# One Strassen level over 1024 tokens: the MLPs of two blocks run as one stage, their hidden values go through DRAM

## Chip, cores, metric

One core of a Trainium2 chip. The time is device microseconds of one launch (us below), median of the runs shown.

## What is computed

One layer of a decoder trunk on 2048 tokens of 1024 features, float32 throughout:

```
h = rms_norm(x, norm_mix);  m = rms_norm(mem, norm_mem)          # x: 2048 x 1024, mem: 256 x 1024
q, k, v, g_lr, r, xq = split(h @ w_in)                             # gated linear attention, 4 heads, chunked, causal
y_mix = rms_norm(attention(q, k, v, decay(g_lr)), out_gain) * silu(r)
y_mem = softmax attention of xq into the memory tokens
x = x + concat(y_mix, y_mem) @ w_out                               # 1536 -> 1024
u = relu(rms_norm(x, norm_mlp) @ w_up)                             # 1024 -> 4096
x = x + (u * u) @ w_down                                           # 4096 -> 1024
out = rms_norm(x, final_norm)
```

## The kernel before

The tokens are worked through in four blocks of 512 (`BLOCKS`, `BLOCK`). A block's **mixers** are the projections, the attention and the output projection; after them comes its **MLP**. All five engines have a program of their own, written out by hand in the order in which the work is to run; they meet at counting semaphores, and each engine takes its instructions strictly in that order. SyncE (SP) issues nearly all DMAs, also in a fixed order, so a DMA behind one whose semaphore is not there yet waits with it.

**Float32 products.** Each operand is split in a high part (`_hi`, ScalarE, ACT below, copies it to the matmul's format) and a low part (`_lo`, VectorE, DVE below, subtracts). A product is then three matmuls, hi x hi, hi x lo, lo x hi (`product`, lines 3026 to 3028). Weights come from DRAM into the two slots of `raw` and are split into the two slots of `w_hi`, `w_lo`.

**Strassen.** With one level of Strassen (Winograd's form) a product of matrices cut in quarters is seven products M1 to M7 of quarters instead of eight. `PRODUCTS` says which operands each takes (A11, A12, A22 and the sums S1 to S4 on the left, B11, B21, B22 and the sums T1 to T4 on the right). M6 is accumulated on M1 in the same PSUM bank, M7 on M6, M4 on M7, and M3 on M5, so a bank has to be read out before the product that goes on in it may start: `empty` is that wait of TensorE (PE below), on `bank_read`.

**The MLP before.** For block 0 `h @ w_up` is done in 16 plain chunks of 256 hidden features (`MLP`, `UPS`). For blocks 1 to 3, 4 chunks are plain and 12 go by Strassen on quarters of 256 tokens ("up a", "up b" in `LATE_MLP`, banks from `late_bank`), which makes matmuls of 256 columns. The hidden values stay on the chip: they are squared, their Strassen sums made (`u_parts`) and split (`u_hi`, `u_lo`), and after each 4 chunks the seven down products of that group follow, by Strassen, in matmuls of 512 columns, each added to `xres` at once (line 2621). The weight sums T1 to T4 of `w_down` are made on the way (`weight_sums`, lines 2087 to 2090) and kept in DRAM (`w_mix`), as are those of `w_up` (`w_up_mix`). The output projection is plain in block 0, by Strassen in the others.

## Time and profile before

| what | value |
|---|---|
| time, median of 3 runs (lowest to highest) | 2464.06 us (2461.39 to 2465.43) |
| span of the profiled execution, first to last instruction | 2459.9 us |
| PE busy | 2441.6 us, 12912 instructions |
| DVE busy | 1830.7 us |
| ACT busy | 1291.8 us |
| DMA moved | 505.00 MB |

The profiled execution has no other time of its own than its span; the 4.2 us from it to the median lie before the first and after the last instruction. An engine's busy time leaves out its waits. A matmul's duration in the profile runs on into the next one's (the array is pipelined), so what one costs PE is read from the distance of starts.

### The profile page before, as it was taken

To read this page: it belongs to the slowest core of one execution; us is meant where nothing else is said; L and a number is where in the kernel's file an instruction comes from. 1 tells how busy PE (TensorE), PEld (TensorE's weight loads), DVE (VectorE), ACT (ScalarE), POOL (GpSimd) and SP (SyncE) were. 2 spreads that over 40 slices of the span, in tenths; PEclk is the share of its full clock that TensorE was granted. 3 is DMA by queue.
4 is the path that set the end of the run, shared out by engine and by line. 5 is a ranking of instruction groups with operands and counts; after the bars stand their busy time and mean duration, and the time that the engine had idled before them with its cause. 6 is when DMAs were issued, how large, how long until landed. Compare 5 with 4: busy or idle time off the path is not lost.

```text
span 2459.9 us, 34497 instructions
## 1 busy us (share of the span) xinstructions
PE 2441.6 (99%) x12912; PEld 2105.9 (86%) x12912; DVE 1830.7 (74%) x2671; ACT 1291.8 (53%) x2035; POOL 312.5 (13%) x327
## 2 busy tenths in 40 slices
PE   9999999999999999999999999999999999999998
PEld 8888888888788888889988888898898888889987
DVE  6677468778856788777775768877785677887777
ACT  5545354544543456566644345665665435556655
POOL 0033200000303320000020431000020142000000
PEclk9999999999999999999999999999999999999999
DMA  8964548677695444466564626355665553545554
GB/s 317 350 213 172 188 172 313 251 274 258 244 373 211 171 163 133 163 214 209 188 219 175 242 101 202 111 184 203 213 212 203 189 199 122 184 149 177 188 182 179
DMA packets 237843, 505.00 MB, mean 205 GB/s; under 512 B 12432, under 2 KB 125456, under 8 KB 219504
## 3 DMA queue, kind: packets, MB, share of 16 engines
q1 hardware_dynamic: 237248, 502.73, 58.4%
q8 instruction: 105, 1.72, 0.3%
q14 instruction: 58, 0.48, 0.1%
q10 hardware_dynamic: 432, 0.07, 0.0%
HBM read 423.07 MB, written 79.69 MB: 204 GB/s over the span
## 4 chain that ended last, share of the span: by engine, by line
PE 95%; DVE 2%; DMA 2%; issue 1%; ACT 0%; POOL 0%; SPq 0%; DVEq 0%; POOLq 0%; ACTq 0%
PE banks L3026 28%; PE banks L3028 28%; PE banks L3027 28%; PE banks L3216 3%; PE banks L3188 1%; PE banks L3262 1%; PE banks L3256 1%; PE banks L3165 1%; PE banks L3240 1%; DMA sr<-in_w_out 1%; PE banks L3178 0%; PE banks L3482 0%; PE banks L3274 0%; DMA xres<-in_x 0%; PE banks L3099 0%
## 5 line engine op out<-in xcount | busy, mean ns | idle before, releaser
L3026 PE MATMUL banks<-h_hi,w_hi 128*128 128x512 f32 (+1 forms) x1728 | 605.6, 350 | 2.4 <-DMA w_lo<-w_in_lo 0.8
L3028 PE MATMUL banks<-h_hi,w_lo 128*128 128x512 f32 (+1 forms) x1728 | 598.1, 346 | 0.0
L3027 PE MATMUL banks<-h_lo,w_hi 128*128 128x512 f32 (+1 forms) x1728 | 597.9, 346 | 0.0
L2833 DVE TENSOR_TENSOR w_lo<-raw,w_hi 128x1024 fp32r<-128x1024 f32 (+1 forms) x312 | 364.8, 1186 | 56.7 <-ACT w_hi L1861 56.4
L1861 ACT ACTIVATE w_hi<-raw 128x1024 fp32r<-128x1024 f32 (+1 forms) x312 | 300.9, 1003 | 166.7 <-PE banks L3026 59.4
L3026 PEld LDWEIGHTS banks<-h_hi,w_hi 128*128 128x128 f32 x1728 | 327.3, 189 | 44.1 <-issue 3.1
L3028 PEld LDWEIGHTS banks<-h_hi,w_lo 128*128 128x128 f32 x1728 | 327.2, 189 | 40.6
L3027 PEld LDWEIGHTS banks<-h_lo,w_hi 128*128 128x128 f32 x1728 | 327.5, 190 | 39.3
L3026 PE MATMUL banks<-w_hi,u_hi 128*128 128x512 f32 x896 | 350.8, 392 | 1.3 <-ACT w_hi L1401 1.0
L3028 PE MATMUL banks<-w_hi,u_lo 128*128 128x512 f32 x896 | 348.8, 389 | 0.0
L3027 PE MATMUL banks<-w_lo,u_hi 128*128 128x512 f32 x896 | 348.7, 389 | 0.0
L2621 DVE TENSOR_TENSOR xres<-banks,xres 128x512 f32<-128x512 f32 x274 | 180.4, 683 | 63.2 <-PE banks L3028 58.8
L3026 PEld LDWEIGHTS banks<-w_hi,u_hi 128*128 128x128 f32 x896 | 168.2, 188 | 40.0 <-issue 4.0
L3028 PEld LDWEIGHTS banks<-w_hi,u_lo 128*128 128x128 f32 x896 | 168.2, 188 | 35.3
L3027 PEld LDWEIGHTS banks<-w_lo,u_hi 128*128 128x128 f32 x896 | 168.2, 188 | 35.0 <-issue 0.7
L2113 DVE TENSOR_TENSOR w_lo<-raw,w_hi 128x1024 fp32r<-128x1024 f32 x116 | 150.0, 1328 | 30.9 <-ACT w_hi L1401 29.3
L1265 POOL TENSOR_TENSOR rstd<-ms,minus_half 128x1 f32<-128x1 f32 x44 | 26.9, 617 | 1146.6 <-DVE ms L2128 1142.2
L2106 DVE TENSOR_TENSOR w_lo<-raw,w_hi 128x2048 fp32r<-128x2048 f32 x47 | 107.7, 2291 | 55.8 <-ACT w_hi L1394 54.8
L1291 POOL TENSOR_TENSOR queries<-q,query_dec 128x384 f32<-128x384 f32 x144 | 120.8, 865 | 182.4 <-ACT query_dec L1557 94.9
L2744 DVE TENSOR_TENSOR u_lo<-u_parts,u_hi 128x768 fp32r<-128x768 f32 (+1 forms) x128 | 135.1, 1092 | 0.8 <-ACT u_hi L1822 0.8
L1401 ACT ACTIVATE w_hi<-raw 128x1024 fp32r<-128x1024 f32 x80 | 81.4, 1053 | 97.6 <-DMA raw<-w_out_mix 31.0
L3026 PE MATMUL banks<-w_hi,h_hi 128*128 128x512 f32 x312 | 126.0, 404 | 1.2 <-ACT v L1527 0.8
(311 smaller groups left out, 4392.9 us busy)
## 6 DMA issues: line engine op xcount, KB each, us to landing
raw<-w_mix SPq DMA_DIRECT2D x52, 1024.0 KB, 4.8
raw<-in_w_down SPq DMA_DIRECT2D x48, 1024.0 KB, 5.7
raw<-w_up_mix SPq DMA_DIRECT2D x72, 512.0 KB, 4.8
w_hi<-w_in_hi SPq DMA_DIRECT2D x29, 1024.0 KB, 4.9
w_lo<-w_in_lo SPq DMA_DIRECT2D x29, 1024.0 KB, 7.9
raw<-in_w_up SPq DMA_DIRECT2D x28, 1024.0 KB, 5.6
raw<-in_gla_w_in SPq DMA_DIRECT2D x21, 1024.0 KB, 7.5
raw<-in_w_up SPq DMA_DIRECT2D x36, 512.0 KB, 4.1
```

The source lines that it names most:

```text
L1291: last = nc.gpsimd.tensor_tensor(kind_cols(queries, w, kind), spans(at_chunk(q, c), w, first, count), kind_cols(query_dec, w, kind), ALU.mult)
L1401: nc.scalar.activation(w_hi[:, i % 2, at], raw[:, i % 2, at], ACT.Copy).then_inc(hi_split.sem, 1)
L1861: nc.scalar.activation(w_hi[:, i % 2, at], raw[:, i % 2, at], ACT.Copy).then_inc(hi_split.sem, 1)
L2106: nc.vector.tensor_tensor(w_lo[:, i % 2, :], raw[:, i % 2, :], w_hi[:, i % 2, :].bitcast(F32), ALU.subtract).then_inc(lo_split.sem, PIECES)
L2113: nc.vector.tensor_tensor(w_lo[:, i % 2, at], raw[:, i % 2, at], w_hi[:, i % 2, at].bitcast(F32), ALU.subtract).then_inc(lo_split.sem, 1)
L2621: nc.vector.tensor_tensor(xres[:, t, cols], bank(name), xres[:, t, cols], ALU.add)\
L2744: nc.vector.tensor_tensor(u_lo[:, c % ring(n), at, :], source, u_hi[:, c % ring(n), at, :].bitcast(F32), ALU.subtract).then_inc(u_ready.se ...
L2833: nc.vector.tensor_tensor(w_lo[:, i % 2, at], raw[:, i % 2, at], w_hi[:, i % 2, at].bitcast(F32), ALU.subtract).then_inc(lo_split.sem, 1)
L3026: after_chunk(pe.matmul(to, left[0], right[0], start=start, stop=False, skip_group_check=goes_on))
L3027: pe.matmul(to, left[0], right[1], start=False, stop=False, skip_group_check=goes_on)
L3028: return pe.matmul(to, left[1], right[0], start=False, stop=stop, skip_group_check=goes_on)
L3216: ins = pe.matmul(bank(name)[:, at:at + cols], keys[:, h, :], queries[:, h, 0:cols], start=True, stop=True)
```

## The change

The program is rewritten around the MLP. The mixers of blocks 0 and 1 now run one after the other, then one MLP for their 1024 tokens; then the same for blocks 2 and 3 (`MLPS` = 2). What it does, part by part:

- **Up.** All 16 chunks go by Strassen, a quarter being 512 tokens x 512 inputs x 128 features, so each of the seven products is 12 matmuls of 512 columns. `UP_STEPS` lists the 112 products (steps): for chunks 0 to 2 first M1 and M2 of each, then M5, M6, and M7, M3, M4; from chunk 3 on M1, M2, M5, M6, M7, M3, M4 of one chunk. The banks are in `up_bank`. The weights' sums are made on the chip from the raw chunk (`up_sum`), each operand is split into one of 8 places (`RING`), five steps ahead.
- **u.** ACT copies M1, M6 and M5 out of their banks (`keep_part`), DVE adds M2, M3 and M7 (`add_part`); relu and square of the three kept quarters is one `scalar_tensor_tensor` each, max(u, 0) * u (`kept_quarters`); the fourth is relu and square on ACT (`last_quarter`). DVE makes S1 to S4 (`u_sums`). All seven operands of the chunk go to DRAM (`u_kept`).
- **Down.** Seven products over all 4096 hidden features in four quarters (`DOWN_STEPS`, 28 steps of 48 matmuls of 512 columns). Each step loads 1 MB of weights and 1 MB of u and splits both.
- **w_down's sums.** 32 halves (`half_mix`) are loaded, summed by DVE between the steps of the first MLP's up part (`DOWN_MIX_AT`) and stored. `w_up_mix` is gone.
- **Mixers.** Block 0's output projection goes by Strassen too. The even block's rows wait in DRAM (`x_kept`), its normed columns too (`h_kept`).

Names in the program rows below: `banks` is PSUM, `s1`..`s4` the sums of h, `part_a`, `part_b`, `part_c`, `gain_fin` the places of a chunk's kept parts.

**PE, before, from the end of M6 (`s2`) to the start of M7 (`s3`) in a Strassen up chunk of blocks 1 to 3:**

```order
L3027 MATMUL banks<-s2_lo,w_hi 128x256
L3028 MATMUL banks<-s2_hi,w_lo 128x256
L3026 MATMUL banks<-s1_hi,w_hi 128x256 [waits bank_read1,s_lo_ready]
...
L3028 MATMUL banks<-s1_hi,w_lo 128x256
L3026 MATMUL banks<-s3_hi,w_hi 128x256 [waits s_lo_ready,bank_read0,lo_split,hi_split]
L3027 MATMUL banks<-s3_lo,w_hi 128x256
```

**PE, after, the same place in a chunk from 3 on:**

```order
L2918 MATMUL banks<-s2_hi,w_hi 128x512
L2919 MATMUL banks<-s2_lo,w_hi 128x512
L2920 MATMUL banks<-s2_hi,w_lo 128x512
L2918 MATMUL banks<-s3_hi,w_hi 128x512 [waits bank_read0,up_lo,up_hi]
L2919 MATMUL banks<-h_lo,w_hi 128x512
L2920 MATMUL banks<-s3_hi,w_lo 128x512
```

Before, M5's 12 matmuls in bank 1 stand between M6 and M7, which share bank 0. Now M7 follows M6 in one bank, and its first matmul waits for one more read of that bank than M6's did, which is ACT's copy of M6.

**DVE, after, at the start of an MLP** (the first row is the sum S1 of h; its waits are for the last transposed columns of h):

```order
L2731 TENSOR_TENSOR s1_sum<-columns_late,a22_sum 128x2048 [waits bank_read2,bank_read3,bank_read5,bank_read4,bank_read7,bank_read6]
L2704 TENSOR_TENSOR w_lo<-third_raw,w_hi 128x512 [waits up_hi]
L2731 TENSOR_TENSOR columns_late<-columns_early,columns_late 128x2048 [waits s_sum_ready,even_low]
L2731 TENSOR_TENSOR columns_early<-s1_sum,columns_early 128x2048 [waits s_sum_ready]
L2704 TENSOR_TENSOR w_lo<-third_raw,w_hi 128x512 [waits up_hi]
L2698 TENSOR_TENSOR third_raw<-third_raw 128x4x128 [waits up_sum_ready] x2
L2749 TENSOR_TENSOR part_a<-banks,part_a 128x512 [waits bank_read0,bank_full6]
L2704 TENSOR_TENSOR w_lo<-raw,w_hi 128x512 [waits up_hi]
L2698 TENSOR_TENSOR raw<-raw 128x4x128 [waits up_sum_ready] x2
L2742 TENSOR_TENSOR s1_lo<-s1_sum,s1_hi 128x2048 [waits s_sum_ready,s_hi_ready]
```

Three sums of 2048 elements now stand ahead of the first add, chunk 0's M2 out of bank 6; chunk 2's M2, the sixth product of the stage, takes bank 6 again. The low part of S1, for the seventh product, comes behind that.

**DVE, after, in the first MLP's up part, between a chunk's add of M2 and its add of M7:**

```order
L2761 SCALAR_TENSOR_TENSOR u<-part_c 128x512 [waits bank_read3]
L2761 SCALAR_TENSOR_TENSOR u<-gain_fin 128x512 [waits bank_read0]
L2096 TENSOR_TENSOR half_mix<-half_mix 128x256 [waits half_mix_loaded0]
L2097 TENSOR_TENSOR half_mix<-half_mix 128x256 [waits dve_step]
L2098 TENSOR_TENSOR half_mix<-half_mix 128x256
L2099 TENSOR_TENSOR half_mix<-half_mix 128x256 [waits dve_step]
L2704 TENSOR_TENSOR w_lo<-raw,w_hi 128x512 [waits up_hi]
L2698 TENSOR_TENSOR raw<-raw 128x4x128 x2
L2773 TENSOR_TENSOR u<-u 128x512 [waits u_sums_stored,relu_ready,square_ready]
L2774 TENSOR_TENSOR u<-u 128x512 [waits dve_step]
L2775 TENSOR_TENSOR u<-u 128x512
L2776 TENSOR_TENSOR u<-u 128x512 [waits dve_step]
```

The squares and sums of the chunk before and a weight sum of `w_down` (four operations) stand in one line with the reads of PSUM.

The diff, cut to its core:

```diff
-PRODUCTS = [("M1", A11, B11, 2, True, (0, 0)), ("M5", S1, T1, 4, True, (1, 1)), ("M6", S2, T2, 2, False, (0, 1)),
...
-LATE_UP_A = (("M1", A11, 0), ("M2", A12, 1), ("M6", S2, 2), ("M5", S1, 3))
-LATE_UP_B = (("M7", S3, 1), ("M3", S4, 0), ("M4", A22, 2))
+MLPS = BLOCKS // 2
+FIRST_UPS = 3
+UP_ORDER = ("M1", "M2", "M5", "M6", "M7", "M3", "M4")
+UP_STEPS = [(c, name) for c in range(FIRST_UPS) for name in ("M1", "M2")]
+UP_STEPS += [(c, name) for name in ("M5", "M6") for c in (2, 1, 0)]
+UP_STEPS += [(c, name) for c in (2, 1, 0) for name in ("M7", "M3", "M4")]
+UP_STEPS += [(c, name) for c in range(FIRST_UPS, UPS) for name in UP_ORDER]
...
+UP_LEAD = 5
...
+UP_ENDS = {15: 2, 20: 1, 25: 0, 30: 3, 36: 4, **{UP_AT[c, "M4"] + 1: c for c in range(5, UPS)}}
+S_SUMS_AT = {0: (S1,), 1: (S3, S2), 3: (S4,)}
+S_LOWS_AT = {2: S1, 4: S2, 5: S3, 7: S4, 9: A22}
...
+DOWN_MIX_AT = {18 + 5 * j // 2: j for j in range(DOWN_MIX)}
...
+def up_bank(c, name):
+    if name == "M2":
+        return 6 + c % 2
+    turn = c if c < FIRST_UPS else (5 - c) % 3
+    return turn + (3 if name in ("M5", "M3") else 0)
...
+            def half_mix_load(j):
+                slot, c, half = j % 2, j // 2, slice(j % 2 * 256, (j % 2 + 1) * 256)
...
+                    sp.wait_ge(half_mix_stored[slot], 16 * (j // 2))
...
+                    if m == 0 and at + 3 in DOWN_MIX_AT:
+                        half_mix_load(DOWN_MIX_AT[at + 3])
+                    if m == 0 and at - 1 in DOWN_MIX_AT:
+                        half_mix_store(DOWN_MIX_AT[at - 1])
...
+                    for e, name in enumerate(("M2", "M3", "M7")):
+                        part = up_home(c, e)
+                        dve.wait_ge(*mlp_read(m, ("up", c, name)))
+                        made = nc.vector.scalar_tensor_tensor(out=u[:, e, :], in0=part, scalar=0.0, in1=part,
+                                                              op0=ALU.max, op1=ALU.mult)
...
+                for at, (c, name) in enumerate(UP_STEPS):
+                    for e in S_SUMS_AT.get(at, ()):
+                        s_sums(e)
+                    if at + UP_LEAD < len(UP_STEPS):
+                        up_low(m, at + UP_LEAD)
+                    if at in S_LOWS_AT:
+                        s_low(S_LOWS_AT[at])
+                    if name in ("M2", "M7", "M3"):
+                        add_part(c, name)
+                    if at - 1 in UP_ENDS:
+                        kept_quarters(UP_ENDS[at - 1])
+                    if at - 2 in UP_ENDS:
+                        u_sums(UP_ENDS[at - 2])
+                    if m == 0 and at in DOWN_MIX_AT:
+                        half_mix_sums(DOWN_MIX_AT[at])
+                kept_quarters(UPS - 1)
+                split_down(0)
+                u_sums(UPS - 1)
...
+            def up_product(s):
+                    c, name = UP_STEPS[s]
...
+                    pe.wait_ge(*mlp_empty(m, ("up", c, name)))
```

By kind, the built programs differ on PE in this: of the matmuls that an operand pair of the split products makes, 3408 have 256 columns before and none after, and the count of those with 512 columns rises by 1500. All other matmuls, the 2688 of the down products among them, keep their number and size.

## Rows read from the trace of the kernel before

**Rows 1.** The page: span, engines' busy time, engines on the chain that ended last.
```profile
span 2459.9 us, 34497 instructions
PE 2441.6 (99%) x12912; PEld 2105.9 (86%) x12912; DVE 1830.7 (74%) x2671; ACT 1291.8 (53%) x2035; POOL 312.5 (13%) x327
PE 95%; DVE 2%; DMA 2%; issue 1%; ACT 0%; POOL 0%; SPq 0%; DVEq 0%; POOLq 0%; ACTq 0%
```

**Rows 2.** Timeline of PE: start and duration in us, engine, line, what.
```profile
1099.71 0.39 PE L3026 MATMUL banks<-w_hi,u_hi 128*128 128x512 f32 x1
...
1102.89 0.39 PE L3028 MATMUL banks<-w_hi,u_lo 128*128 128x512 f32 x1
1103.11 0.28 PE L3026 MATMUL banks<-h_hi,w_hi 128*128 128x256 f32 x1
...
1113.07 0.28 PE L3028 MATMUL banks<-h_hi,w_lo 128*128 128x256 f32 x1
```

**Rows 3.** Timeline: a product's last matmul and the first read of its bank, twice.
```profile
1117.38 0.28 PE L3028 MATMUL banks<-s_hi,w_lo 128*128 128x256 f32 x1
...
1117.77 0.38 ACT L1877 ACTIVATE c_parts<-banks 128x256 f32<-128x256 f32 x1 [0.28 <-PE banks L3028]
...
2452.98 0.39 PE L3028 MATMUL banks<-w_hi,u_lo 128*128 128x512 f32 x1
...
2453.40 0.69 DVE L2621 TENSOR_TENSOR xres<-banks,xres 128x512 f32<-128x512 f32 x1
```

**Rows 4.** ACT reading PSUM: the group of 512 elements, and eight reads of 256.
```profile
L1520 ACT ACTIVATE xq_a<-banks 128x512 f32<-128x512 f32 x16 | 9.6, 598 | 56.3 <-PE banks L3028 56.3
...
944.70 3.03 ACT L1775 ACTIVATE h_hi<-banks,gain_mlp 128x256 fp32r<-128x256 f32 x8 [2.12 <-PE banks L3482]
```

**Rows 5.** Timeline: PE starting again behind a releaser, in brackets the idle time.
```profile
395.37 0.47 PE L3026 MATMUL banks<-w_hi,u_hi 128*128 128x512 f32 x1 [0.98 <-ACT w_hi L1401]
...
709.61 0.20 ACT L1527 ACTIVATION_READ_ACCUMULATOR v<-banks,neg_top 128x1 f32 x1
...
709.95 1.32 PE L3165 MATMUL banks<-kmT,xq_a 128*128 128x256 f32 x5 [1.55 <-ACT v L1527]
```

**Rows 6.** DVE by shape: count, busy us, mean ns, idle before.
```profile
L2833 DVE TENSOR_TENSOR w_lo<-raw,w_hi 128x512 fp32r<-128x512 f32 x36 | 24.5, 680 | 0.0
L2732 DVE TENSOR_TENSOR u_parts<-u_parts 128x256 f32<-128x256 f32 x64 | 26.7, 418 | 0.0
L2426 DVE SCALAR_TENSOR_TENSOR sr<-b,sr 128x512 f32<-128x512 f32 x16 | 10.8, 676 | 46.2 <-ACT sr L1620 46.2
L2363 DVE TENSOR_TENSOR v_s<-raw,v_s 128x2048 fp32r<-128x2048 f32 x4 | 9.1, 2282 | 0.0
```

**Rows 7.** Timeline of DVE: two splits of 1024, then operations of 512.
```profile
560.55 2.35 DVE L2113 TENSOR_TENSOR w_lo<-raw,w_hi 128x1024 fp32r<-128x1024 f32 x2
562.82 0.68 DVE L2087 TENSOR_TENSOR xin<-xin 128x512 f32<-128x512 f32 x1
563.53 0.69 DVE L2088 TENSOR_TENSOR xin<-xin 128x512 f32<-128x512 f32 x1
564.14 0.69 DVE L2089 TENSOR_TENSOR xin<-xin 128x512 f32<-128x512 f32 x1
```

**Rows 8.** Chain in order of time: the 16 transposes of one half of h.
```profile
935.43 1.75 PE banks L3482 x16
```

**Rows 9.** DMA issues: count, KB each, median us from issue to landing.
```profile
raw<-in_w_up SPq DMA_DIRECT2D x36, 256.0 KB, 2.8
w_up_mix<-gain_fin SPq DMA_DIRECT2D x11, 512.0 KB, 4.1
w_in_lo<-w_lo SPq DMA_DIRECT2D x13, 1024.0 KB, 11.2
```

**Rows 10.** Windows: us; PE, PEld, DVE, ACT, POOL busy; granted clock; DMA share, GB/s.
```profile
2456.00:2458.00 2.00, 0.00 (x0) 0.00 (x0) 1.41 (x2) 0.00 (x0) 0.00 (x0) 0.99 0.82 334
2458.00:2460.00 2.00, 0.00 (x0) 0.00 (x0) 0.00 (x0) 0.00 (x0) 0.00 (x0) 0.50 0.50 191
```

More of the change, by code:

```diff
@@ L281, in block_uses @@
         if hs < 8:
[L282 removed]
+            if hs // 2 % 2 == 0 and not v_by_sums(n):
                 for t in v_tiles(hs):
@@ L738, in build, with bank_count @@
         dve_step = sem("dve_step")
         ones_r = ones[:].bitcast(F32R)
-        def bank_count(n, name, more):
-            uses = layout(n).uses
-            bank, index = uses.place[name]
-            ahead = sum(layout(m).uses.count[bank] for m in range(n))
+        def bank_count(phase, name, more):
+            bank, index = USES[phase].place[name]
+            ahead = sum(USES[before].count[bank] for before in range(phase))
             return bank, EARLY.count[bank] + ahead + index + more
@@ L864, in mix_uses @@
         def mix_uses(j):
-            return sum(mix_slot(before) == mix_slot(j) for before in range(j))
-        def slot_uses(slot, n, steps=None):
-            return sum(mix_slot(j) == slot for j in range(steps or MIX_STEPS + (OUT_MIX if n else 0)))
-        def mlp_source(s):
-            if MLP[s][0] == "up":
-                return wup[:, :, FCOLS * MLP[s][1]:FCOLS * (MLP[s][1] + 1)], KD
-            g, operand = MLP[s][1], PRODUCTS[MLP[s][2]][2]
+            return sum(OUT_MIX_SLOT[before] == OUT_MIX_SLOT[j] for before in range(j))
@@ new lines, in slot_uses, with columns, up_load, up_parts @@
+        def slot_uses(slot):
+            return OUT_MIX_SLOT.count(slot)
+        def columns(b):
+            return columns_late if b == 2 else columns_early
+        def up_load(c):
+            return sum(up_slot(before) == up_slot(c) for before in range(c))
+        def up_parts(c):
+            return third_parts if c == 2 else raw_parts[:, c % 2]
+        def up_source(c, operand):
+            k, f = {B11: (0, 0), B21: (1, 0), B22: (1, 1), T1: (0, 0), T3: (0, 1), T2: (0, 0), T4: (1, 0)}[operand]
+            return up_parts(c)[:, KG * k:KG * (k + 1), f, :]
@@ new lines, in store_rows, with store_columns @@
+            def store_rows(n):
+                for pair in range(2):
+                    sp.wait_ge(*read(n, ("out", "M4", pair)))
+                sp.dma_start(x_kept[:, n % 2, :, :], xres[:]).then_inc(rows_stored.sem, 16)
+            def store_columns(n):
+                for half in range(2):
+                    for g in range(KD // 2):
+                        sp.wait_ge(*read(n + 1, ("kept hT", half, g)))
+                sp.dma_start(h_kept, columns_early[:]).then_inc(columns_stored.sem, 16)
@@ L2056, in _ @@
+                for t in range(TILES):
+                    act.wait_ge(*mlp_read(m, ("down", "M4", t)))
+                    if m < MLPS - 1:
+                        square(ends[1][:, t, :], "final", m, TILES + t)
                     else:
                         half_square(t, 0)
+            for n in range(BLOCKS):
+                mixers(n)
+                if n % 2:
+                    mlp(n // 2)
         @block.vector
@@ L2211, in _, with mixers @@
             dve.wait_ge(half_gain_ready, 1)
-            for n in range(BLOCKS):
-                c_mlp, chunks = enter_block(n)
-                c_out, c_r = layout(n).out, layout(n).r
+            def mixers(n):
+                enter(mixers_phase(n))
+                c_end, c_out, c_r = layout(n).end, layout(n).out, layout(n).r
                 def next_chunk(i):
-                    if n and c_out <= i + 1 < c_mlp:
+                    if i + 1 >= c_out:
                         split_lo_out(n, i + 1)
@@ L3010, in _ @@
+                restart()
+            for n in range(BLOCKS):
+                mixers(n)
+                if n % 2:
+                    mlp(n // 2)
         @block.tensor
```

2687 lines of the change are left out of this document (1236 added, 1451 removed).

## The prediction

> **What bounds the kernel now.** I read the page first, for who sets the end. PE is busy 2441.6 of 2459.9 us and 95% of the chain that ended last is PE [rows 1]; DVE has 74%, ACT 53%. So a change pays only through what PE has to do, and costs through every wait that it gives PE. There is little old waiting to win back: PE's own idle time is 18 us, of which about 7 us stand behind its last matmul, at 2452.98 [rows 1, 3]. Next I read PE's timeline for the price of a matmul, from start to start, since the durations overlap: 14 intervals of 512 columns take 1102.89 - 1099.71 = 3.18 us, 0.227 us each; 83 of 256 columns take 9.96 us, 0.120 us each [rows 2]. Two matmuls of 256 cost 0.240 us, so one of 512 is 5% cheaper than its halves.
>
> **Matmuls.** 3408 of 256 columns go: 3408 x 0.120 = 409.0 us. 1500 of 512 come: 340.5 us. The difference is **-68.5 us**. (In short: three quarters of the up part had the Strassen saving already, at half the width; the rest, and block 0's output projection, get it now.) PE would be busy for about 2373 us.
>
> The Trainium skill ("TensorE: Matmul & The Clock Gate", section "Wait — 56ns, not 53.3ns?") gives N / 2.4 GHz and some 2.5 ns on top for the distance of two starts: 215.7 ns for 512 and 109.2 ns for 256. By that the difference would be 323.6 - 372.2 = -48.6 us, and the total below 20 us higher, no change. By that rule the trace does not agree: the distances are 11 ns longer at either width, and that part falls away with each of 1908 matmuls fewer.
>
> **New wait 1: M7 behind M6 in one bank.** From chunk 3 on M7 goes on in the bank in which M6 has just ended, and ACT must copy M6 out in between (the program rows in the section on the change). Before, M5 stood there. From the start of M6's last matmul to ACT's copy: 1117.38 to 1117.77, 0.39, and with 512 columns 2452.98 to 2453.40, 0.42 us [rows 3]. The copy of 512 elements: 0.60 us [rows 4]. From ACT's end (709.61 + 0.20) to PE's start: 0.14 us [rows 5]. Such a first matmul lasts 0.47 for 0.39 us: 0.07 more [rows 2, 5]. Of the sum, 1.23, the usual 0.227 goes off: 1.0 us. It comes 13 times in each MLP: **+26 us**. Bounds: 0.85 us if the copy runs like the shortest reads of PSUM on ACT (3.03 / 8 = 0.38 us for 256 elements [rows 4] leaves little below 0.45 for 512), and 1.1 if ACT is just in another copy: 22 to 29 us.
>
> **New wait 2: the start of an MLP.** Take the start of the first product as 0; a product lasts 12 x 0.227 = 2.72 us. After two products PE makes the second half of h's columns, 16 transposes in 1.75 us [rows 8], from 5.4 on. ACT reads these banks, eight reads in 3.03 us [rows 4], until about 9.0. Only then may DVE start S1: 2048 elements, 2.28 us [rows 6], to 11.3. In DVE's order follow a split of 512 (0.6 by distance of starts, 562.82 to 564.14 is 0.61 to 0.71 [rows 7]), S3 and S2 (2 x 2.28), another split, two weight sums (1.33, as two operations of 512 [rows 6]): 18.4. Then the add of chunk 0's M2, out of bank 6, to 19.0. The sixth product, chunk 2's M2, wants bank 6 at 5 x 2.72 + 2.0 = 15.6 us: late by 3.5 us. It ends at 21.9; the seventh needs the low part of S1, which is behind one more split and two sums and itself takes 2.28: 23.2. Late again, 1.4 us. Together 4.9 us, two MLPs: **+9.8 us**. Bounds 0 (if ACT's reads and the split end so much earlier that the order slips in) and 8 us each (each of the 2048s at its dearest, and DVE not through with the mixers).
>
> **New wait 3: up to down.** Behind chunk 15's M3, DVE has the add (0.6), the three squares (3 x 0.61 = 1.83) and only then the first split of the down part, 2 x 1.135 us [rows 7]: with 0.5 for the start some 5.3 us. PE has only M4 in between and wants the first down product at 2.95: 2.3 us, twice: **+4.6 us**.
>
> **DVE in the first MLP's up part.** Per chunk DVE has 7 splits (4.2), 4 weight sums (2.55), 3 adds (1.8), 3 squares (1.83), 4 sums of u (2.66): 13.0 us in a period of 7 x 2.72 + 1.0 = 20.1. A half of w_down's sums is four operations of 256 elements, 0.42 busy in the mean [rows 6], between 0.34 and 0.455 by whether each waits for the one before: 1.59 us; 2.8 of them fall in a chunk: 17.5 us. That fits, 87%, but not at every place. Between the reads of M2 and M7 there can be the squares, two halves and u's sums: then M7's read is done at about 19.0 where PE wants that bank at 17.75, 1.3 us, and some 0.45 with one half. Averaged over the orders 0.8 us a chunk in 11 chunks: **+9 us**. Bounds 0 (the second MLP has none, and its chunks should show it) and 25 (1.3 us at both places in most of the chunks).
>
> **What lies hidden.** A down step is 48 matmuls, 10.9 us; DVE splits in it for 4 x 1.135 = 4.5 us and ACT needs about as much, and its two loads of 1 MB, bounded by the slowest row, 11.2 us for 1 MB [rows 9], are issued some 9 us or more before they are used and behind each other; with the faster rows (2.8 us for 256 KB, 4.1 for 512 KB) they have room. Without that cover each step would cost a few us. I take 0, up to +10. The two joins of the mixers with the even block's rows in DRAM: +2, the old waits at places that vanish: -2 (PE's largest ones of before were near 1 to 2 us each [rows 5]). The tail behind the last matmul stays.
>
> **The sum.** -68.5 + 26 + 9.8 + 4.6 + 9 + 2 - 2 = -19.1 us, from the span 2459.9 to 2440.8. The profiled execution's span lies 4.2 us under the median of the runs, and the same lies around it after: 2445.0 us. **2445 us**, -0.8%.
>
> **Rivals.**
> - *The waits are smaller (faster by far).* If S1 comes early enough, half sums slip into DVE's gaps, and only M7's wait stays, at its low bound: -68.5 + 22 + about 2 = -44.5, a median near 2420 us. For it: DVE has 13% to spare even in the first MLP. Against it: my walk puts DVE over 3 us late at one named place.
> - *The halves' round trip (slower).* Two slots of `half_mix` serve 32 halves, a new one each 2.5 products. A slot must be summed, stored, the store awaited by SP, loaded again, summed: two spacings, 5 x 2.72 = 13.6 us and a share of M7's wait, 14.9. With 1.6 for the sums and landings like 2.8 and 4.1 us [rows 9], and their issues at the steps' turns, some 11 us: fits. With a store and a load like the 11.2 us row the trip takes some 17.5 us, and it decides from 15 to 16 on. DVE waits in its strict order, with PSUM reads queued behind, and the program waits on the rest: about 2.8 us for each pair of halves, 16 pairs, +45 us, with M7's and the other waits a median near 2490 us. For it: SP is strict too, and a store's wait stops all loads of weights behind it. Against it: the halves are 0.5 MB or less a piece, and DMA moves only 505 MB in 2464 us in the whole program before.
> - *PE's clock.* In the last two windows the granted clock is 0.99 from 2456 to 2458 and 0.50 (the 1.2 GHz level) from 2458 to 2460, with PE idle since 2453.4 [rows 3, 10]. If it falls in the 3.5 us of waiting at an MLP's start too, the matmuls behind take twice their 0.227 us until it is back. No row shows for how long; for two products (24 matmuls) it is 5.4 us, in two places +11: 2456 us. Against it: PE idles less there than ahead of the fall in the rows.
> - *The wide matmul costs more in the up part.* If its distance there is just two of the narrow one's, 0.240 us, nothing is gained by width: 1500 x 0.013 = +20 us, 2465 us. Against it: the 0.227 us, in the down part, with the same operand types [rows 2].
> - *Joins.* Loads of even rows, h's operands out of DRAM and the first down operands each late by some us, 20 us in all beyond the sum: about 2465 us, no change.
>
> **From cases to numbers.** The likeliest case, the sum as it stands with each wait within its bounds, 0.58 (its own range 2432 to 2457). Smaller waits 0.14; round trip 0.12; clock 0.07; wide matmul 0.02; joins 0.07. What a measurement of this kernel can tell from no change is about 0.2%, 5 us: 2459 to 2469. Faster: 0.58 + 0.14 + 0.05 of the clock's + 0.03 of the joins' = 0.80. Same: 0.02 of the clock's + 0.02 of the wide matmul's + 0.03 of the joins' = 0.07. Slower: 0.12 + 0.01 = 0.13. The range: up to 2466 it leaves out the round trip and little of the joins, down to 2422 half of the smaller waits' case: 0.8 in it.
>
> **What would show it.** Right: PE idle about 1 us, 26 times, before M7's first matmul, with ACT's copy of M6 as the releaser; about 3.5 and 1.4 us at each MLP's start, ended by DVE's add and by S1's low part; about 2.3 us at each down part's start; chunks of the first MLP longer than the second's by nearly 1 us, DVE over 85% busy there; PE busy near 2373 us. Down steps of 10.9 us without idle time. Wrong: waits of DVE for half_mix's load over 1 us (round trip), granted clock under 1 inside the up part, idle PE before down products with a DMA as the releaser, or a 512-column distance other than 0.227 us, of which each 0.01 us is some 15 us in the difference.

## The result, and the profile after

The changed kernel takes 2506.97 us (median of 4 runs, 2502.8 to 2509.44) against 2462.72 (2459.51 to 2465.43) for the one before on the same chip: ratio 1.0176, 95% interval 1.0161 to 1.0191. It is 1.8% slower; the forecast was 2445 us, in a range of 2422 to 2466.

The page of the changed kernel: span, busy time, chain.

```profile
span 2503.2 us, 29903 instructions
PE 2404.3 (96%) x11004; PEld 1991.1 (80%) x11004; DVE 1657.8 (66%) x2476; ACT 1068.1 (43%) x1794; POOL 349.4 (14%) x341
PE 57%; DVE 3%; DMA 2%; issue 1%; ACT 1%; SPq 0%; POOL 0%; DVEq 0%; ACTq 0%
```

Beside [rows 1], PE is busy for less, 2404 us for 2442, but it is 57% of the chain that ended last and not 95%. Its waits by releaser (us in total, times, longest) come to 85 us in these rows; in the same view of the kernel before, all of PE's waits come to 11.1 us:

```profile
PE banks L2918 <- ACT part_c L1964: 25.2, 14, 6.8
PE banks L2918 <- ACT part_a L1964: 23.6, 12, 6.3
PE banks L2918 <- issue: 10.9, 7, 3.1
PE banks L2918 <- DVE part_a L2749: 7.6, 2, 3.8
PE banks L2918 <- ACT w_hi L1986: 4.7, 2, 2.3
PE banks L2918 <- DVE xres L2619: 4.4, 5, 1.1
PE banks L3113 <- ACT v L1595: 4.4, 1, 4.4
PE banks L2918 <- DVE y_sum_lo L2534: 3.0, 2, 1.5
PE banks L2918 <- DVE part_b L2749: 1.4, 3, 0.8
```

**The matmuls came as forecast.** In both traces 512 columns are 0.227 us apart and 256 columns 0.120, and a product of the up part without a wait takes the 2.72 us of the forecast. From the two timelines: PE's last matmul starts 41.6 us later (2494.62 against 2452.98 [rows 3]), its listed idle time grows by 79.4 us (90.5 against 11.1) and the time that matmuls take beyond their usual distance by 32.9 us. So the matmuls themselves give 41.6 - 79.4 - 32.9 = -70.7 us; the forecast had -68.5. This is an estimate: the last term comes out at 31 to 36 us by how it is counted.

**The two MLPs differ.** I measure the up part from the start of the sixth product, behind the wait at the MLP's start, to the first down product: 353.8 us in the first MLP (637.41 to 991.18), 310.3 in the second (1878.17 to 2188.51), for the same work of PE. Windows over the two (columns: us; PE, PEld, DVE, ACT, POOL busy; granted clock; DMA share, GB/s):

```profile
637.00:992.00 355.00, 312.99 (x1288) 251.57 (x1289) 263.37 (x455) 114.08 (x191) 0.00 (x0) 0.94 0.67 225
1878.00:2189.00 311.00, 297.26 (x1285) 241.36 (x1286) 213.44 (x326) 114.80 (x190) 0.00 (x0) 0.99 0.42 149
```

Only the first has the halves of `w_down`'s sums. DVE is busy for 74% of that stretch, not 87%: it waits, for the loads of the halves (us in total, times, longest):

```profile
DVE half_mix L2096 <- DMA half_mix<-in_w_down: 62.2, 19, 6.1
```

The timelines around 742 us show a wait that is handed on (idle time and releaser in brackets). DVE's:

```profile
737.15 0.43 DVE L2096 TENSOR_TENSOR half_mix<-half_mix 128x256 f32<-128x256 f32 x1 [5.04 <-DMA half_mix<-in_w_down]
...
740.55 1.29 DVE L2698 TENSOR_TENSOR raw<-raw 128x512 f32<-128x512 f32 x2
```

ACT's, next:

```profile
741.36 0.63 ACT L1941 ACTIVATE w_hi<-raw 128x512 fp32r<-128x512 f32 x1 [7.61 <-DVE raw L2698]
741.89 0.58 ACT L1964 ACTIVATE part_c<-banks 128x512 f32<-128x512 f32 x1
```

And PE's:

```profile
742.62 0.77 PE L2918 MATMUL banks<-s_hi,w_hi 128*128 128x512 f32 x1 [6.85 <-ACT part_c L1964]
743.18 0.63 PE L2919 MATMUL banks<-h_lo,w_hi 128*128 128x512 f32 x1
743.60 0.63 PE L2920 MATMUL banks<-s_hi,w_lo 128*128 128x512 f32 x1
```

DVE waits 5.0 us for a half's load. Behind it in DVE's list stand the weight sums of `raw`; for those ACT's next split waits 7.6 us, and behind that split in ACT's list stands the copy of M6, for which PE's M7 waits 6.85 us. The row names the copy as the releaser, but it is the last link of a chain that begins at a DMA. Why the load is late is seen on SP. Its timeline (start, time of issuing; in a row with x2 from the first issue to the end of the second):

```profile
732.54 1.20 SPq L1057 DMA_DIRECT2D half_mix<-in_w_down  x2
733.79 0.60 SPq L1173 DMA_DIRECT2D u_kept<-u  x1
734.43 0.51 SPq L1065 DMA_DIRECT2D w_mix<-half_mix  x1
741.12 1.20 SPq L1057 DMA_DIRECT2D half_mix<-in_w_down  x2
```

Its waits from 690 to 985 us, by releaser:

```profile
SPq L1057 <- DMA w_mix<-half_mix: 150.0, 29, 9.6
SPq L1169 <- DVE u L2761: 31.4, 8, 13.6
```

The issues of DMAs from 690 to 960 us (count, KB, median us to landing):

```profile
w_mix<-half_mix SPq DMA_DIRECT2D x30, 512.0 KB, 6.2
half_mix<-in_w_down SPq DMA_DIRECT2D x58, 256.0 KB, 3.7
```

SP issues a half's store, then waits for that store's landing, because the next load in its list goes to the same slot: 29 waits, 150 us. Loads' issue 1.2, a store of u 0.6, the half's store's issue 0.5 and its landing 6.2 stand in series: 8.5 us for this half (7.9 where no store of u lies between), and 2.5 products take 6.8.

**The clock.** Behind such waits PE runs for a while at nearly twice its distances: in the rows from 743.18 on above starts are 0.42 us apart and not 0.227. Windows of the changed kernel (columns as above), around the waits of 4.4 us at 135, 3.8 at 637 and 3.1 at 1557:

```profile
130.00:140.00 10.00, 5.62 (x20) 4.58 (x20) 7.04 (x12) 5.22 (x9) 3.75 (x4) 0.68 0.49 179
630.00:640.00 10.00, 6.20 (x25) 4.77 (x25) 9.90 (x11) 6.41 (x7) 0.00 (x0) 0.94 0.00 0
640.00:650.00 10.00, 10.00 (x40) 7.70 (x40) 9.96 (x10) 6.58 (x8) 0.00 (x0) 0.89 0.00 0
1550.00:1560.00 10.00, 5.69 (x19) 4.38 (x20) 10.00 (x7) 3.67 (x5) 10.00 (x5) 0.85 0.26 97
```

The mean granted clock over the span is 0.986 (before: 1.000). PE's busy time shows it too: 2404.3 us, 31 more than the forecast's 2373. Of the 32.9 us beyond the usual distances, the first MLP's up part has some 15 more than the second's.

**Two waits in the mixers that the forecast did not have.** In block 0, ACT's timeline:

```profile
124.72 1.08 ACT L1508 ACTIVATE junk<-second_rows 128x1024 bf16<-128x1024 f32 x1
...
129.35 0.40 ACT L1642 ACTIVATE diag<-y_rows 128x256 fp32r<-128x256 f32 x1
```

PE's behind it:

```profile
135.26 0.77 PE L3113 MATMUL banks<-diag,ones 128*128 128x256 f32 x2 [4.38 <-ACT v L1595]
```

Four squares of block 1's rows, 4.7 us, stand ahead of `diag` and the first decays; before, the same place had none. And in the output projection of blocks 0 and 2, first POOL's timeline:

```profile
297.56 16.33 POOL L1338 TENSOR_TENSOR columns_early<-columns_early,rows_next 128x512 f32<-128x512 f32 x8
```

DVE's, ahead of it and beside it:

```profile
291.07 1.22 DVE L2534 TENSOR_TENSOR y_sum_lo<-y_sum,y_hi_b 128x1024 fp32r<-128x1024 f32 x1
...
302.09 2.30 DVE L2534 TENSOR_TENSOR y_sum_lo<-y_sum,y_hi_q 128x1024 fp32r<-128x1024 f32 x1
```

PE's:

```profile
304.54 0.47 PE L2918 MATMUL banks<-w_hi,y_hi_q 128*128 128x512 f32 x1 [1.50 <-DVE y_sum_lo L2534]
310.62 0.47 PE L2918 MATMUL banks<-w_hi,y_hi_q 128*128 128x512 f32 x1 [3.10 <-issue]
```

The same DVE operation takes 1.22 us alone and 2.30 beside POOL's scaling of the next block's columns.

The Trainium skill ("SBUF — State Buffer", section "SBUF: two separate sides") says that a DVE operation with two SBUF inputs and a GpSimd operation that reads SBUF lock a shared pair of ports against each other for whole instructions. With that rule the trace agrees: both operations here read SBUF, the DVE operation twice, and it takes 2.30 us for 1.22.

### The profile page after: what moved, and what is told of

Read it like the earlier page. It is cut to its first block, busy times and chain, and to the rows that moved or that the text cites. A ratio compares the mean times of both kernels' runs of the same rounds, so it can differ in the third digit from the quotient of the medians.

```text
span 2503.2 us, 29903 instructions
## 1 busy us (share of the span) xinstructions
PE 2404.3 (96%) x11004; PEld 1991.1 (80%) x11004; DVE 1657.8 (66%) x2476; ACT 1068.1 (43%) x1794; POOL 349.4 (14%) x341
## 4 chain that ended last, share of the span: by engine, by line
PE 57%; DVE 3%; DMA 2%; issue 1%; ACT 1%; SPq 0%; POOL 0%; DVEq 0%; ACTq 0%
PE banks L2918 18%; PE banks L2920 17%; PE banks L2919 17%; DMA w_mix<-half_mix 2%; PE banks L3129 1%; DVE w_lo L2119 1%; DMA raw<-in_w_out 1%; PE banks L3101 1%; PE banks L3175 1%; PE banks L3169 1%; PE banks L3078 0%; PE banks L3153 0%; DVE xres L2619 0%; PE banks L2967 0%; ACT part_c L1964 0%
## 5 line engine op out<-in xcount | busy, mean ns | idle before, releaser
L2918 PE MATMUL banks<-h_hi,w_hi 128*128 128x512 f32 x896 | 356.8, 398 | 2.4 <-DVE part_b L2749 1.4
L2919 PE MATMUL banks<-h_lo,w_hi 128*128 128x512 f32 x896 | 354.3, 395 | 0.0
L2920 PE MATMUL banks<-h_hi,w_lo 128*128 128x512 f32 x896 | 349.1, 390 | 0.0
L2918 PE MATMUL banks<-s_hi,w_hi 128*128 128x512 f32 x512 | 208.2, 407 | 48.8 <-ACT part_c L1964 25.2
L2920 PE MATMUL banks<-s_hi,w_lo 128*128 128x512 f32 x512 | 205.1, 400 | 0.0
L2918 PEld LDWEIGHTS banks<-h_hi,w_hi 128*128 128x128 f32 x896 | 168.3, 188 | 38.9 <-ACT w_hi L1941 3.8
L2919 PEld LDWEIGHTS banks<-h_lo,w_hi 128*128 128x128 f32 x896 | 171.8, 192 | 34.1
L2920 PEld LDWEIGHTS banks<-h_hi,w_lo 128*128 128x128 f32 x896 | 168.2, 188 | 35.7
L2919 PE MATMUL banks<-s_lo,w_hi 128*128 128x512 f32 x384 | 149.6, 390 | 0.0
L2791 DVE TENSOR_TENSOR u_lo<-u_raw,u_hi 128x1024 fp32r<-128x1024 f32 x112 | 140.9, 1258 | 9.8 <-ACT u_hi L1997 9.8
```

The costliest lines, as they stand in the source:

```text
L2791: nc.vector.tensor_tensor(u_lo[slot][:, at, :], u_raw[slot][:, at, :], u_hi[slot][:, at, :].bitcast(F32), ALU.subtract).then_inc(u_lo_read ...
L2918: after_chunk(pe.matmul(to, left[0], right[0], start=start, stop=False, skip_group_check=goes_on))
L2919: pe.matmul(to, left[0], right[1], start=False, stop=False, skip_group_check=goes_on)
L2920: return pe.matmul(to, left[1], right[0], start=False, stop=stop, skip_group_check=goes_on)
```

## The experiments

Times are medians; ratios are to the kernel before, on the same chip, with 95% intervals. "Section" is the up part as above, in the first and the second MLP. The runs stand on several chips, and the kernel before took 2460.5 to 2463.2 us on them, so a difference between two runs of the changed program, as given below, is good to some 2 us. Runs that leave out halves, stores or the scaling compute another result; they are for the time alone. GpSimd in the expectations is POOL.

### The stores ahead of the loads, in SP's list

```diff
-                    if m == 0 and at + 3 in DOWN_MIX_AT:
-                        half_mix_load(DOWN_MIX_AT[at + 3])
                     if m == 0 and at - 1 in DOWN_MIX_AT:
                         half_mix_store(DOWN_MIX_AT[at - 1])
+                    if m == 0 and at + 2 in DOWN_MIX_AT:
+                        half_mix_load(DOWN_MIX_AT[at + 2])
```

> SyncE's list alone is changed: a half's store stands ahead of the load of the half after next, and that load comes two steps ahead of its sum instead of three. Theory A (SyncE's strict order: a load that waits for a store's landing holds back the next store, so every half costs a landing in series): the waits for half_mix go, PE's waits before M7 in the first MLP fall back to 0.84 us each, and the clock stays up there; 2507 - 27 of waits - 15 of clock, about 2465 us (2462 to 2475). Theory B (the transfers themselves are too slow, 1 KB rows on busy DMA engines): nothing gained, 2495 to 2515 us, DVE's waits for half_mix's load remain over 3 us. Theory C (DVE has too much work): unchanged, 2507 us.

2487.22 us, 1.0104 (1.0088 to 1.0121); sections 332.9 and 310.3. Half of what theory A wanted. SP's waits for landings fell from 150 to 12.7 us, so the order was part of it; but DVE still waited 24.8 us for loads, now issued a step later, and SP waited 54 us for DVE's sums in their place. The store's landing got shorter too (690 to 940 us; 6.2 before):

```profile
w_mix<-half_mix SPq DMA_DIRECT2D x30, 512.0 KB, 3.6
```

And this beside more traffic, 265 GB/s in that stretch where the changed kernel has 244: behind the loads of the other slot a store took 6.2 us, ahead of them 3.6.

### Without the halves

```diff
-                    if m == 0 and at in DOWN_MIX_AT:
-                        half_mix_sums(DOWN_MIX_AT[at])
...
-                return w_mix[:, quarter, operand - T1, :, :]
+                operand = (B11, B21, B22, B21)[operand - T1]
```

> Leaves out the 32 half sums of w_down altogether (their loads, sums and stores); the down part loads rows of w_down in place of the sums. All theories: the first MLP's up part becomes like the second's, 353.8 - 43.4 = 310.3 us from the sixth product to the first down product, and the time 2507 - 43 = about 2464 us. If the first MLP stays longer than the second, something other than the halves is late there.

2463.47 us, 1.0008 (0.9999 to 1.0018); sections 311.2 and 310.4. The halves cost 43.5 us (by the ratios 41, by the sections 42.6). All three theories had this.

### The halves' sums alone

```diff
+                    if m == 0 and DOWN_MIX_AT.get(at + 3, 2) < 2:
+                        half_mix_load(DOWN_MIX_AT[at + 3])
...
-                    dve.wait_ge(half_mix_loaded[j % 2], 32 * (j // 2 + 1))
+                    dve.wait_ge(half_mix_loaded[j % 2], 32)
```

> Leaves out 30 of the 32 loads and all 32 stores of the half sums, but keeps all 32 sums on DVE in their places (on data already there); the down part loads rows of w_down in place of the sums. This is DVE's share alone. Theories A and B: near the kernel without any halves, plus what the prediction put on DVE's time (0 to 9 us): 2464 to 2475 us. Theory C: it stays at 2495 us or more.

2468.77 us, 1.0026 (1.0016 to 1.0036); sections 316.2 and 311.3. DVE's own share is 5 us; theory C falls. The other 38 us are loads and stores.

### M5 between M6 and M7

```diff
-UP_STEPS += [(c, name) for c in range(FIRST_UPS, UPS) for name in UP_ORDER]
+UP_STEPS += [(c, name) for c in range(FIRST_UPS, UPS) for name in ("M1", "M2", "M6", "M5", "M7", "M3", "M4")]
...
+                        if e == T2:
+                            to, a, b = b11, b12, b11
+                        if e == T1:
+                            to, a, b = b11, b22, b11
```

> From chunk 3 on the order is M1, M2, M6, M5, M7, M3, M4, with the weights' sums made in another order (T3, T2, then T4, T1), so that M5 stands between M6 and M7 as before the change. Theory: the 26 waits of 1.0 us are ACT's copy of M6 in between; all 13 of the second MLP go (-13 us), in the first those that hold no longer wait go, and the long ones there shorten by up to 2.7 us since M7's copy has a product more: 2507 - 20 to - 45, about 2478 us. Rival (ACT's copies come late for another reason, its splits or the sums it waits for): the waits stay where they are, 2500 us or more.

2489.06 us, 1.0109 (1.0092 to 1.0126); sections 353.0 and 296.0. In the second MLP 14.3 us go, about the 13 waits before M7 at 1.12 us each (1.00 up to M7's first matmul, 0.12 up to the next). So the copy of M6 is the cause there. In the first MLP nothing goes: its pace is that of the halves, and the waits moved to other products (3.5 us at 721.64, 3.8 at 742.02). The whole gained 17.9 us, a little under the range expected.

### The squares early

```diff
+                    if n == 0 and i == C_V - 1:
+                        act.wait_ge(second_rows_loaded, 16 * 2)
+                        for t in range(TILES):
+                            square(second_rows[:, t, :] if t < 3 else second_last[:, 0, :], "next", 1, t)
                     attention_exp(i - C_Q)
...
-                    if n == 0 and i == C_V - 1:
```

> ScalarE's four sums of squares for block 1 in block 0's mixers stand ahead of its last attention step, in a gap of 6.6 us that it has there, in place of right behind it, ahead of the first decays. Theory: they are the cause of PE's wait of 4.4 us at 135 us and of the low clock behind it (granted clock 0.68 in 130 to 140): both go, -7 us, about 2500 us. Rival: the decays wait for something else there, and the time stays at 2507 us (within 2).

2500.95 us, 1.0152 (1.0137 to 1.0167): -6.0 us; the wait of 4.4 us is gone, and the granted clock in 120 to 140 us is 1.00.

### The loads on POOL's queue

```diff
+                if m == 0:
+                    for j in range(DOWN_MIX):
+                        half_mix_load(j)
```

> The 32 halves of w_down are loaded from GpSimd's queue, which has nothing else to do there, and each load waits only for its slot's store; the stores stay in SyncE's list. Theory A (SyncE's strict order makes the halves late; in the run with the stores first, its waits for u took their place): the waits for half_mix go and the first MLP's up section falls from 353.8 to what it took with the sums alone, 316 us: 2507 - 38, about 2469 us. Theory B (the transfers are slow by themselves, with this traffic): DVE still waits for the loads, section above 330 us, time above 2480 us.

2481.11 us, 1.0079 (1.0061 to 1.0096); sections 327.2 and 310.4. Between the theories. The loads now waited on POOL for the stores' landings, 199.6 us in 29 waits, the longest 24.3, because the stores still stood in SP's list behind its waits for u and for DVE's sums.

### Loads on POOL's queue, M5 between, squares early

The edits of three of the runs above in one kernel.

> Three edits together: the halves loaded from GpSimd's queue, M6 ahead of M5 from chunk 3 on, the squares early. If the three causes are apart and the order of M6 and M5 hides its copy in the first MLP too once the halves come in time: 2507 - 38 (halves) - 28 (M7's waits, both MLPs) - 7 (squares) = about 2434 us, 1.1% under the kernel before. If DVE's work of 87% of a now shorter period stands in the way in the first MLP, some 5 to 10 us more.

2460.78 us, 0.9993 (0.9984 to 1.0003); sections 329.0 and 296.8. A miss by 27 us, and no difference from the kernel before. The first MLP did not gain from the order of M6 and M5; that the halves set its pace was argued here, and the run without halves below shows it.

### Without POOL's scaling

```diff
-                    nc.gpsimd.tensor_tensor(columns(b)[:, k, :], columns(b)[:, k, :], rows_next[:], ALU.mult)\
+                    nc.gpsimd.tensor_tensor(columns(b)[:, k, 0:8], columns(b)[:, k, 0:8], rows_next[:, 0:8], ALU.mult)\
```

> GpSimd's eight multiplications of the next blocks' columns (2 us each, beside the output projection of blocks 0 and 2) work on 8 of the 512 elements of each row; the rest of the scaling is left out. Theory: DVE's splits of 1024 take twice their 1.22 us while they run, and that makes PE's waits of 1.5, 3.1 and 1.1 us in the output projections of blocks 0 and 2: those go, with the low clock behind them, 2507 - 15 = about 2492 us. Rival: the projections of even blocks lack their weights for another reason (loads, y's sums): the waits stay, 2505 us or more.

2494.11 us, 1.0124 (1.0109 to 1.0139): -12.9 us. The waits of 1.5 and 3.1 us are gone in both places, and all 16 `y_sum_lo` operations take 1.22 us.

### Both on POOL's queue, one half in flight

```diff
+                    for j in range(DOWN_MIX):
+                        half_mix_store(j)
+                        if 2 <= j + 1 < DOWN_MIX:
+                            half_mix_load(j + 1)
```

> Loads and stores of the halves both leave SyncE's list for GpSimd's queue, in the order store j, then load j+1; nothing else is changed. With the loads alone moved, each still waited for a store that stood in SyncE's list behind waits of up to 13 us for u. Theory A (a strict list ahead of the halves' DMAs, and no more): DVE's waits for half_mix's load go, the section of the first MLP comes to 316 us as with the sums alone, 2507 - 37 = about 2470 us. Theory B (the 1 KB rows are slow by themselves beside the other traffic): DVE's waits for the loads stay near 25 us in sum, section 325 to 330 us, 2480 us.

2526.16 us, 1.0260 (1.0242 to 1.0278); section 374.8 in the first MLP. A clear miss: in this order a load is issued only once the half before has been summed, so sum, issues and landing stand in series, about 8.4 us for each half. The same with M5 between M6 and M7 and the squares early:

> The same move of the halves, with M6 ahead of M5 from chunk 3 on and the squares early. Against the run with the loads alone on GpSimd's queue (2461, section 329.0): the section falls by what the moved stores give, to between 305 and 320 us, and the time to about 2445 us. If DVE (17.5 us of work in a period that is now 19.0) is the bound there and not the queue, it stays over 320 us and 2452 us.

2498.91 us, 1.0147 (1.0132 to 1.0162); section 366.6: the same fault, 54 us over what was expected. The same again with the sums' places at `18 + 21 * j // 8`:

> As the run with both on GpSimd's queue, M6 ahead of M5 and the squares early, but the 32 sums stand 2.625 products apart in place of 2.5, to leave loads and DVE more time for each. If the transfers' time is what is short, 3 to 8 us less than that run; if DVE's total work is, the same; if only single places collide, other ones do now, within 3 us of it.

2494.73 us, 1.0130 (1.0115 to 1.0146); section 363.2. More room for each half gave 4.2 us, as its first case had it; the order of waiting stayed.

### Both on POOL's queue, store j, then load j + 2

```diff
-                        if 2 <= j + 1 < DOWN_MIX:
-                            half_mix_load(j + 1)
+                        if j + 2 < DOWN_MIX:
+                            half_mix_load(j + 2)
```

> Loads and stores of the halves both on GpSimd's queue, as in the run that took 2526 us, but in the order store j, then load j+2 (which waits for that store's landing), so that the load of the next half is already under way. In series for each half are now a store's issue (0.8), its landing (3.4) and two loads' issue (1.4): 5.6 us, under the 6.8 us of 2.5 products; in the other order it was sum, store's issue, loads' issue, landing of the loads: 1.6 + 0.8 + 1.4 + 4.6 = 8.4 us. Theory A (order of waiting): DVE's waits for the loads fall under 15 us in sum, first MLP's section 316 to 322 us, 2470 to 2476 us. Theory B (transfers): 330 us and 2485 us or more.

2492.41 us, 1.0125 (1.0112 to 1.0138); section 339.3. Better by 34 us than the other order, but by its numbers theory B and not A. Behind the loads of the other slot the store's landing took 5.7 us in the median, not 3.4, and issue, landing and issue in series 7.9 us, again over 6.8. With the other edits and the sums 2.625 products apart:

> The same order, with M6 ahead of M5 from chunk 3 on, the squares early and the sums 2.625 products apart. Against the run in the other order (2494.7, section 363): theory A: section 300 to 315 us and 2432 to 2447 us, faster than the kernel before by about 1%. Theory B: section 325 us or more, 2457 us or more.

2460.34 us, 0.9992 (0.9983 to 1.0002); sections 332.6 and 295.8. Theory B's numbers again. The next two experiments decide between the amount of data and the waiting.

### Without the stores

```diff
-                    if m == 0 and at - 1 in DOWN_MIX_AT:
-                        half_mix_store(DOWN_MIX_AT[at - 1])
...
-                    sp.wait_ge(half_mix_stored[slot], 16 * (j // 2))
+                    sp.wait_ge(half_mix_made, j - 1)
```

> Leaves out the 32 stores of the half sums; a load waits for its slot's sum in place of the store's landing, in the same place of SyncE's list; the down part loads rows of w_down in place of the sums. Loads (16 MB) and sums stay. Theory D (the slot's trip: sum, store's issue and landing, loads' issue and landing, near 13.2 us by the medians of the changed kernel's trace, against 13.6 for two halves): without the store's 6.7 us it has room, DVE's waits for the loads go under 5 us, the first MLP's section falls from 353.8 to 316 us, 2507 - 37 = about 2470 us. Theory B (the loads are slow beside the other traffic, or stand behind SyncE's waits for u): DVE goes on waiting, section over 325 us, 2480 us or more.

2468.05 us, 1.0032 (1.0019 to 1.0045); sections 316.6 and 310.3. Theory D: loads and sums cost no more than the sums alone, so the 38 us come with the stores. Waiting for their landing and their 16 MB are gone together here; the run with three slots parts them. And the kernel without halves, with M5 between M6 and M7 and the squares early:

> Leaves out the halves altogether, as the run that took 2463.5 us, with M6 ahead of M5 from chunk 3 on and the squares of block 1 early. If the three causes are apart: 2463.5 - 28 (two MLPs' waits before M7 at 14.3 each, as measured in the second MLP) - 6 (squares) = about 2429 us, both sections near 296 us. If something else takes the place of M7's waits in the first MLP, its section stays above 300 us.

2427.67 us, 0.9866 (0.9850 to 0.9883); both sections 295.7. The three causes add up, and without the halves the first MLP gains from the order as the second does.

### Three slots

```diff
+        mixes = [(half_mix[:, 0, 0:2, :], half_mix[:, 0, 2:4, :]), (half_mix[:, 1, 0:2, :], half_mix[:, 1, 2:4, :]),
+                 (rows_next[:].rearrange("p (e c) -> p e c", e=2), gain_fin[:, BLOCK:D].rearrange("p (e c) -> p e c", e=2))]
...
-                    sp.wait_ge(half_mix_stored[slot], 16 * (j // 2))
+                    sp.wait_ge(half_mix_stored[slot], 32 * (j // 3))
```

> All loads, sums and stores of the halves stay, in SyncE's list as changed, but in three slots in place of two (the third in tiles that are idle in the first MLP), each half as two stores. Theory D (the slot's trip of 13 to 14 us against 13.6): with 20.4 us for it the waits go, DVE's waits for the loads under 8 us in sum, first MLP's section 316 to 320 us, 2507 - 36 = about 2471 us. Theory B (16 MB in and 16 MB out are too much beside the other traffic there): DVE waits on, section over 328 us, 2482 us or more.

2470.05 us, 1.0034 (1.0023 to 1.0046); sections 316.4 and 310.5. Nothing is left out here. DVE's waits for the loads in the first MLP:

```profile
DVE half_mix L2100 <- DMA half_mix<-in_w_down: 2.8, 3, 1.4
```

And SP's for the landings:

```profile
SPq L1059 <- DMA w_mix<-half_mix: 1.5, 1, 1.5
SPq L1059 <- DMA w_mix<-gain_fin: 0.8, 2, 0.4
```

Of 62 and 150 us, 3 and 2 are left, with every byte still moved: it was the landing in series, not the amount of data. Two things are not parted. The stores are cut in two here, and a half-size store landed in 2.6 to 3.6 us. And a third slot gives room both to SP's list and to the trip of one slot (load, sum, store, landing); the run with the stores first, which freed the list alone, brought the section from 353.8 to 332.9, this one to 316.4. With M5 between M6 and M7 and the squares early as well:

> Three slots, M6 ahead of M5 from chunk 3 on, the squares early; nothing is left out. From the run without the halves (2427.7) plus the halves' cost: DVE's own work took 5 us in a period of 20 us, in one of 19 it is dearer, 5 to 12 us; 2433 to 2445 us, most likely 2438, faster than the kernel before by 1%. Theory B, or DVE as the bound: over 2452 us.

2450.10 us, 0.9950 (0.9937 to 0.9962); sections 317.5 and 297.0. Faster than the kernel before, but between the two theories: the first MLP still gained nothing from the order. PE's waits there, one in each chunk, 1.1 us in most and up to 2.7, now end with ACT's `w_hi`.

### The halves at chosen places

```diff
-DOWN_MIX_AT = {18 + 5 * j // 2: j for j in range(DOWN_MIX)}
+DOWN_MIX_AT = {21 + 7 * (j // 3) + (0, 3, 5)[j % 3]: j for j in range(DOWN_MIX)}
```

> As the run with three slots, M6 ahead of M5 and the squares early (2450.1 us), but the halves' sums stand at three fixed places of each chunk (with M1, M5 and M3), none in the steps of M2 and M6, where DVE has 3.0 and 4.6 us of other work for a product of 2.72. Theory P (places collide: ScalarE's next split waits for a weight sum behind a half): the waits of 1.1 us twice per chunk and of 1.6 to 2.7 us go, section 298 to 307 us, 2431 to 2440 us. Theory C (DVE's total work): section stays at 315 us or more, 2448 us.

2439.01 us, 0.9913 (0.9899 to 0.9926); sections 309.1 and 295.9. This is the fastest complete kernel, 0.9% under the one before. The places gave 11 us (by the ratios 9): the waits of 1.6 to 2.7 us went, and the time is theory P's, though the section is 2 us over its range. The waits of 1.1 us, one a chunk and not two as the expectation had them, stayed in most chunks (PE's timeline):

```profile
752.93 0.47 PE L2933 MATMUL banks<-h_hi,w_hi 128*128 128x512 f32 x1 [1.11 <-ACT w_hi L1946]
773.36 0.47 PE L2933 MATMUL banks<-h_hi,w_hi 128*128 128x512 f32 x1 [1.11 <-ACT w_hi L1946]
```

Whether these are DVE's total work or one more place was not tried.

## Why the prediction was wrong

Its working, step by step:

- **Matmuls, -68.5.** Right: about -70.7 from the timelines. The Trainium skill's distances ("TensorE: Matmul & The Clock Gate", section "Wait — 56ns, not 53.3ns?"), by which -48.6 would have come, are not what either trace shows: 0.227 us for 512 columns, not 0.216.
- **M7 behind M6, 1.0 us x 26.** The cause is right, the size a little short. Timeline of the changed kernel, second MLP:

```profile
2176.50 0.39 PE L2920 MATMUL banks<-s_hi,w_lo 128*128 128x512 f32 x1
2177.73 0.47 PE L2918 MATMUL banks<-s_hi,w_hi 128*128 128x512 f32 x1 [0.84 <-ACT part_c L1964]
...
2178.26 0.40 PE L2920 MATMUL banks<-s_hi,w_lo 128*128 128x512 f32 x1
```

  From the last matmul of M6 to this one are 1.23 us, 1.00 more than a usual distance, and the starts behind it come another 0.12 late: 1.12 us, 14.6 in one MLP where 13 were forecast. That the 1.23 is met exactly is luck: the working had in it 0.07 us for the longer first matmul, which comes behind that start. The experiment took 14.3 us out of the second MLP.
- **The start of an MLP, 4.9 us x 2.** Idle 3.80 us where 3.5 were forecast, with DVE's add as the releaser. The 1.4 us behind it did not come as a wait: the granted clock fell behind the first wait in both MLPs, the rival that had 0.07, and the sixth product took 4.2 to 4.3 us for 2.72, so that S1's low part, ready at 641.4 and 1882.2 us, was hardly late. With what stands around the two, an MLP's start cost 5.8 and 5.6 us for 4.9: the fall was real, but most of it lay over a wait that was there anyway.
- **Up to down, 2.3 us x 2.** Idle 2.34, twice.
- **"DVE in the first MLP's up part", +9.** This is the step that failed. As DVE's time it was nearly right (5.3 us by the sums alone). But it counted only DVE's time for a half and put the waits for its DMAs at nothing; the halves cost 43.5 us, 34 more than forecast. The DMAs stood only in the rival of the round trip, with 0.12. It had the waiting for the store's landing right and the condition wrong: it compared one slot's trip with two spacings (11 against 14.9 us) and did not follow the order of SP's list, in which each store's landing stands in series with the next load and the next store, one landing for each spacing of 6.8 us. The 14.9 is long by its own terms: 13.6 and five sevenths of M7's 1.0 us are 14.3. Its landings, 2.8 and 4.1 us [rows 9], were short for the store, which took 6.2. Traffic does not explain this: where the stores of 4.1 us stood (425 to 608 us) the kernel before moved 259 GB/s, the changed one moves 243 among the halves. It goes with the place in the queue: behind the other slot's loads the store took 6.2 and 5.7 us in two runs, ahead of them 3.6 and 3.4. The rival's price, +45 us, came out close to the 43.5 by a sum of other terms, which is luck; its sign, waits of DVE for a half's load over 1 us, was the right one to look for.
- **Joins, +2 - 2.** The squares cost 6.0 us, POOL's scaling 12.9, neither in the forecast. The first could be read in the order of ACT's instructions. The second could not be read in [rows 7], where POOL is idle beside DVE.

Of 62 us of error 34 are the halves, 6 the squares, 13 the scaling; the 9 that are left were not split up by runs (by estimate some 3 are M7's waits and 2 the MLPs' starts; the clock at the second down part's start and smaller joins are in the rest). The chances were too sure: 0.80 for faster rested on the sum's having all its terms.

## What to carry to other kernels

A load that reuses a buffer waits for the store's landing out of it; in a queue that is served strictly in order, add up, for each item, everything that is waited for in series, and compare it with the time between two items. Take a landing from a row that stands in the same place of its queue: the same store took 3.4 to 6.2 us by what was issued ahead of it and beside it. One more buffer, with the stores cut in two, was worth 37 us (by the ratios 35); other orders and queues gave from a loss of 19 to a gain of 26. Where a wait's releaser is cheap and early in its own right, follow its engine's list back to the instruction ahead of it that waited: here a copy was named, and a DMA two engines away was late. And take the order of every engine, not only of those that the change is about: the squares and the scaling were small moves in stages that it was not about.

## What the runs showed of the hardware

DVE operations of 1024 elements with two operands in SBUF took 1.22 us alone and up to 2.31 beside POOL's multiplications of 512 elements. In the profiled execution of the changed kernel PE's granted clock fell at each of the 11 single waits of 3.1 us and more (0.68 to 0.94 in the windows above), and at two of the four of 2.3 to 2.6 us; in that of the kernel before, with no wait over 2.11 us ahead of the end, it was 1.000. A store of 512 KB landed in 6.2 us (median) where it was issued right behind two loads, and in 3.6 where it went ahead of them, with more traffic beside it.
